# Input projection of a hybrid decoder: ten of thirteen tiles as Strassen pairs

## The chip, the cores and the metric

One core of a Trainium2 chip runs the whole program. The metric is the device time of one execution in microseconds (us), the median of several. TensorE multiplies matrices (PE in the profile; PEld is its weight load), VectorE (DVE), ScalarE (ACT) and GpSimd (POOL) do the elementwise work, SyncE (SP) issues most DMAs. Every engine works through its own queue in order and waits on semaphores. All data is float32.

## The reference

One inference step of a decoder trunk with 1024 prompt tokens and 8 sample tokens, 1032 in all. First the tokens are normalised, `xn = x * rsqrt(mean(x*x) + eps) * norm_g`, and projected, `u = xn @ w_in`, with 1024 input features. The first 1664 columns of `u` are `z`, the input of the RWKV branch:

```
zm = z + mu * (z_prev - z)
r, k, v, wl, al = split(zm)        # 512, 512, 512, 64, 64 columns
w_raw = -softplus(-(w0 + tanh(wl) @ w_b)) - 0.5
```

`z_prev` is `z` of the token before (zero before the first prompt token, a stored row for each sample token). The last row of `z` of the prompt and the rows of the samples, before mixing, are outputs. The RWKV recurrence, the sparse attention, the merge of the two and the rest of the trunk follow; the change doesn't touch them.

## The kernel before

The kernel is a row of stages, each ended by a barrier of all engines. The change is in the first, `project_input`, which makes `z` for all tokens, transposed: features on the 128 partitions, tokens along the free dimension. `zT` holds 13 tiles of 128 features by 1032 tokens. `Z_TILES` is the order of the tiles: tile 12 (the LoRA inputs wl and al) first, then k, r and v of each head pair.

The tokens arrive as nine tiles (eight of 128, one of 8). ACT sums the squares (L617) and takes the root, DVE scales the tile (L664), TensorE transposes it (`turn`, L552), eight transposes a tile, and ACT (L607) and DVE (L654) each copy half of the result out of PSUM into `xnT` and multiply it by the gain. ACT and DVE work in the order: square or scale tile i, then copy out tile i-1.

A product (`product`, L566) is one tile of `zT` for one third of the tokens: eight matmul calls, one for each 128 input features, 344 columns each. In float32 every call becomes two instructions, so 16 instructions in a product and 39 products in all. The order is

```
order = ([(n, g) for g in range(3) for n in range(Z_FIRST)] + [(n, g) for n in range(Z_FIRST, ZT) for g in range(3)])
```

with `Z_FIRST` = 4 (L431, L438): column group 0 of the first four tiles, then group 1, then group 2, while the later tokens are still on their way, and after those tile by tile. Behind each of the first six products stands the transposing of one token tile (L552), behind the ninth that of the stored shift rows (L584). Six PSUM banks go round; ACT copies each product out (L628) and, when a tile is complete, its last nine columns into `zlast` (L634).

The weights of a tile (`w_z`, 512 KB) come by DMA into a ring of four; SP asks for tile n when tile n-4 is done (`weights`, L491). POOL makes the difference `z_prev - z` of a complete tile (L538 to L540) and DVE mixes it in (L682). When all tiles are saved, TensorE transposes the 13 pieces of `zlast` (L589), ACT copies the rows out (L638), and SP stores them. The next stage, `rwkv_prompt`, begins with its LoRA products (L856, L858) and fills TensorE's gaps with the columns of the other branches (L845).

A much later stage, `merge_branches` (L2698 on), already computes its gates in quarter products: L2819 are its matmuls, L2835 ACT's copies, L2892 DVE's adds out of PSUM, L2860 the sums of weights and L2869 the sums of inputs, L2936 an addition on POOL.

Of the kernel before, what the change touches and what calls it, by code (L numbers as in the profile page):

```python
# [15 lines left out]
ALU = mybir.AluOpType  # L16
# [3 lines left out]
P = 128  # L20
# [410 lines left out]
Z_FIRST = 4  # L431
# [3 lines left out]
def project_input(nc, k, x, o):  # L435

    ring, w_ring = 4, 4
    order = ([(n, g) for g in range(3) for n in range(Z_FIRST)] + [(n, g) for n in range(Z_FIRST, ZT) for g in range(3)])  # L438
    place = {ng: u for u, ng in enumerate(order)}
    done_at = [1 + max(place[n, g] for g in range(3)) for n in range(ZT)]  # L440
    with Stage(nc) as ctx:
# [10 lines left out]
        d = sb("z_diff", [P, ring, TT])  # L452
        root_first = sb("root_first", [P, 1])
# [9 lines left out]
        diffed, mixed, lora_in = ctx.sem("z_diffed"), ctx.sem("z_mixed"), ctx.sem("tanh_done")  # L463
        block = ctx.enter_context(nc.Block())
# [20 lines left out]

        def turn_bank(i):
# [36 lines left out]
        def _(pool):  # L523
# [9 lines left out]
            for n, t in enumerate(Z_TILES):  # L533
                if n >= ring:
                    pool.wait_ge(mixed, n - ring + 1)
                pool.wait_ge(copied, done_at[n])
                s = d[:, n % ring, :]
                nc.gpsimd.tensor_scalar(s[:, 0:1], k.zT[:, t, 0:1], -1.0, None, ALU.mult).then_inc(diffed, 1)  # L538
                nc.gpsimd.tensor_tensor(s[:, 1:NP], k.zT[:, t, 0:NP - 1], k.zT[:, t, 1:NP], ALU.subtract).then_inc(diffed, 1)
                nc.gpsimd.tensor_tensor(s[:, NP:TT], st[:, t, :], k.zT[:, t, NP:TT], ALU.subtract).then_inc(diffed, 1)  # L540

        @block.tensor
        def _(pe):
# [12 lines left out]
            def product(u):  # L556
                n, g = order[u]
                if g == 0 or u >= 3 * Z_FIRST:
                    pe.wait_ge(in_w[n % w_ring], 16 * (n // w_ring + 1))
# [8 lines left out]
                last.then_inc(summed, 1)  # L568

# [6 lines left out]
            for u in range(len(order)):  # L576
                product(u)
                if u + 3 <= NT:
                    turn(u + 3)
                if u == NT:  # L580
                    pe.wait_ge(in_st, 16)
                    pe.wait_ge(out_v, NT + 1)
                    for t in range(ZT):
                        last = nc.tensor.transpose(k.ps[:, 7, t * NB:(t + 1) * NB], st_rows[:, t * P:(t + 1) * P],  # L584
                                                   k.ident[0:NB, 0:NB])
                    last.then_inc(st_t, 1)
            pe.wait_ge(saved, ZT)
            for t in range(ZT):
                last = nc.tensor.transpose(k.ps[0:NB + 1, t // 4, (t % 4) * P:(t % 4 + 1) * P], zlast[:, t, :],  # L589
                                           k.ident[:])  # L590
            last.then_inc(last_t, 1)

        @block.scalar
        def _(act):
# [31 lines left out]
            for u, (n, g) in enumerate(order):  # L626
                act.wait_ge(summed, u + 1)
                nc.scalar.activation(k.zT[:, Z_TILES[n], g * CG:(g + 1) * CG], k.ps[:, u % 6, 0:CG], ACT.Copy).then_inc(copied, 1)  # L628
                if g == 2:
                    act.wait_ge(copied, u + 1)  # L630
                    if n == Z_FIRST + 2:
                        act.wait_ge(mixed, 1)
                        nc.scalar.activation(k.zT[0:HD, ZT - 1, :], k.zT[0:HD, ZT - 1, :], ACT.Tanh).then_inc(lora_in, 1)
                    nc.scalar.activation(zlast[:, Z_TILES[n], :], k.zT[:, Z_TILES[n], NP - 1:TT], ACT.Copy).then_inc(saved, 1)  # L634
            act.wait_ge(last_t, 1)
            for b in range(4):
                n = min(4, ZT - 4 * b) * P
                nc.scalar.activation(k.last_rows[:, b * 512:b * 512 + n], k.ps[0:NB + 1, b, 0:n],  # L638
# [4 lines left out]
        def _(dve):  # L643
# [13 lines left out]

            dve.wait_ge(vec_o, 1)
# [11 lines left out]
            turned_out(NT)  # L670
            nc.vector.tensor_scalar(k.omka[:], k.vec[:, V_KA:V_KA + NPAIR], -1.0, 1.0, ALU.mult, ALU.add).then_inc(vec_o, 1)
# [7 lines left out]
            for n, t in enumerate(Z_TILES):  # L679
                dve.wait_ge(saved, n + 1)  # L680
                dve.wait_ge(diffed, 3 * n + 3)
                nc.vector.scalar_tensor_tensor(out=k.zT[:, t, :], in0=d[:, n % ring, :],  # L682
                                               scalar=k.vec[:, V_MU + t:V_MU + t + 1], in1=k.zT[:, t, :],
                                               op0=ALU.mult, op1=ALU.add).then_inc(mixed, 1)
# [2947 lines left out]
```

## Time and profile before

| | us |
|---|---|
| three timed runs | 1788.53, 1781.71, 1786.95 |
| their median | 1786.95 |
| the profiled execution | 1775.88 |
| its span in the profile | 1774.1 |
| TensorE busy (share of the span) | 1690.9 (95%) |
| DVE, ACT, POOL busy | 814.6, 577.2, 376.7 |
| matmuls of L566 busy | 182.0 |

The profile shows one execution. Busy time of TensorE counts the time in which at least one matmul is under way; matmuls overlap, so the mean length of one (453 ns for 344 columns) is longer than the step from one to the next. A row of the timeline gives the start, the length, the engine, the line, the operation with what it writes and reads, and in brackets how long the engine had been idle and what released it.

### The profile page before, as it was taken

What the parts mean: (1) busy time and instruction counts of PE and PEld (TensorE: products, weight loads), DVE (VectorE), ACT (ScalarE), POOL (GpSimd) and SP (SyncE); (2) the same over time, 40 slices, a digit from 0 to 9 for tenths busy, and PEclk for the clock granted to TensorE, in tenths of its full rate; (3) what the DMA queues carried; (4) which work ended last, traced back from release to release, by engine and by line L of the source; (5) the groups of instructions that cost most, each with busy time, mean ns of one, the idle gap of its engine ahead of it and who ended that gap; (6) DMA issues with size and microseconds to landing.
All of it is one profiled execution on the core that took longest, in us unless ns stands there. A gap on an engine that the chain in (4) does not pass through costs nothing. (4 is left out here: it accounts for less than half of the span.)

```text
span 1774.1 us, 40928 instructions
## 1 busy us (share of the span) xinstructions
PE 1690.9 (95%) x17848; PEld 1157.7 (65%) x17848; DVE 814.6 (46%) x1684; ACT 577.2 (33%) x1229; POOL 376.7 (21%) x442
## 2 busy tenths in 40 slices
PE   7999889999999989999999899899999999899997
PEld 5666566666666645667666689776568888545443
DVE  3100165455545419077666666272133356633444
ACT  4111245344343211276666221113322221111444
POOL 0211233232212100055655322103300013100110
PEclk9999899999999999999999899899999999999999
DMA  4112001000100045091200497529720141510001
GB/s 159 48 36 54 2 3 27 14 15 15 26 15 15 15 125 74 1 251 49 96 2 1 125 306 285 173 77 214 189 52 24 48 142 25 220 42 1 24 24 48
DMA packets 115463, 135.88 MB, mean 77 GB/s; under 512 B 48252, under 2 KB 97093, under 8 KB 110334
## 3 DMA queue, kind: packets, MB, share of 16 engines
q1 hardware_dynamic: 106034, 83.97, 17.2%
q0 software_dynamic: 9216, 49.29, 9.0%
q8 instruction: 142, 2.33, 0.6%
q14 instruction: 35, 0.29, 0.1%
q10 hardware_dynamic: 36, 0.01, 0.0%
HBM read 120.64 MB, written 16.62 MB: 77 GB/s over the span
## 5 line engine op out<-in xcount | busy, mean ns | idle before, releaser
L845 PE MATMUL ps<-xnT,rw_side_w 128*128 128x344 f32 x576 | 204.0, 479 | 0.0
L566 PE MATMUL ps<-xnT,w_z 128*128 128x344 f32 x624 | 182.0, 453 | 2.3 <-DVE xnT L654 1.3
L566 PEld LDWEIGHTS ps<-xnT,w_z 128*128 128x128 f32 x624 | 117.9, 190 | 62.9 <-issue 1.5
L1965 POOL TENSOR_SCALAR probs<-probs,row_sums,gates 128x63 f32<-128x63 f32 (+6 forms) x148 | 95.6, 662 | 229.8 <-DVE row_sums L1921 229.3
L845 PEld LDWEIGHTS ps<-xnT,rw_side_w 128*128 128x128 f32 x576 | 99.2, 191 | 40.3 <-issue 3.3
L2232 PE MATMUL ps<-xnT,zT 128*128 128x344 f32 x384 | 120.8, 463 | 0.0
L2232 PEld LDWEIGHTS ps<-xnT,zT 128*128 128x128 f32 x384 | 71.7, 194 | 36.0 <-issue 5.6
L278 PE MATMUL ps<-w_kv,xnT 128*128 128x396 f32 x256 | 89.6, 509 | 3.5 <-DMA w_kv<-in_w_in_dram 3.4
L1870 ACT ACTIVATE probs<-probs,neg_max 128x63 f32<-128x63 f32 (+6 forms) x148 | 87.5, 595 | 1.5 <-DVE neg_max L1911 1.5
L1817 PE MATMUL ps<-kT,zT 64*128 64x512 f32 (+3 forms) x384 | 73.7, 496 | 2.6 <-PEq L82 1.4
L278 PEld LDWEIGHTS ps<-w_kv,xnT 128*128 128x128 f32 x256 | 48.8, 194 | 40.7 <-DMA w_kv<-in_w_in_dram 7.8
L1844 PE MATMUL ps<-probsT,kvtok 128*64 128x128 f32 x1056 | 75.3, 280 | 0.0
L682 DVE SCALAR_TENSOR_TENSOR zT<-z_diff,vec,zT 128x1032 f32<-128x1032 f32 x13 | 16.8, 1294 | 126.2 <-POOL z_diff L540 113.5
L1830 PE MATMUL ps<-ident,probs 128*128 128x128 f32 (+1 forms) x460 | 68.1, 280 | 5.1 <-DVE probsT L1942 3.4
L1886 ACT ACTIVATE probsT<-ps 128x512 f32<-128x512 f32 (+1 forms) x80 | 45.9, 574 | 82.6 <-PE ps L1830 82.6
L1844 PEld LDWEIGHTS ps<-probsT,kvtok 128*64 128x64 f32 x1056 | 56.0, 136 | 24.0 <-issue 23.0
L2936 POOL TENSOR_TENSOR mT<-mT,gate_n 128x258 f32<-128x258 f32 x28 | 23.7, 854 | 218.0 <-DVE gate_n L2899 218.0
L1344 POOL TENSOR_TENSOR rw_Lb<-rw_Lm,level_mask 128x512 f32<-128x512 f32 x40 | 53.9, 1355 | 63.8 <-DVE rw_Lm L1513 38.8
L1942 DVE COPY probsT<-ps 128x512 f32<-128x512 f32 (+1 forms) x80 | 50.5, 632 | 36.0 <-PE ps L1830 35.1
L2835 ACT ACTIVATE zT<-ps 128x258 f32<-128x258 f32 x72 | 27.8, 387 | 109.0 <-PE ps L2819 86.2
L1830 PEld LDWEIGHTS ps<-ident,probs 128*128 128x128 f32 (+1 forms) x460 | 49.8, 140 | 17.9 <-issue 10.5
L628 ACT ACTIVATE zT<-ps 128x344 f32<-128x344 f32 x39 | 17.3, 464 | 132.7 <-PE ps L566 132.7
(560 smaller groups left out, 3263.7 us busy)
## 6 DMA issues: line engine op xcount, KB each, us to landing
w_z<-in_w_in_dram SPq DMA_DIRECT2D x13, 512.0 KB, 3.8
xnT_kept<-xnT SPq DMA_DIRECT2D x1, 4128.0 KB
x_tok<-in_x_prompt_dram SPq DMA_DIRECT2D x8, 512.0 KB
rw_side_w<-in_w_in_dram SPq DMA_DIRECT2D x16, 256.0 KB, 3.3
zT<-in_w_in_dram SPq DMA_DIRECT2D x8, 512.0 KB, 5.3
ring_k<-in_w_in_dram SPq DMA_DIRECT2D x8, 512.0 KB, 5.3
w_out<-in_w_out_dram SPq DMA_DIRECT2D x1, 4096.0 KB
h_tok<-in_x_prompt_dram SPq DMA_DIRECT2D x8, 512.0 KB, 8.4
```

Source lines behind the costliest of these rows:

```text
L278: last = nc.tensor.matmul(k.ps[:, u % 4, 0:half], k.xnT[:, c, i * P:(i + 1) * P], w[:, c, h * half:(h + 1) * half], start=(c == 0), stop=( ...
L566: last = nc.tensor.matmul(k.ps[:, u % 6, 0:CG], w[:, n % w_ring, c, :], k.xnT[:, c, g * CG:(g + 1) * CG], start=(c == 0), stop=(c == KC - 1))
L845: ins = nc.tensor.matmul(k.ps[:, SIDE_BANKS[g % 2], 0:CG], w.side[:, t % 2, c, :], k.xnT[:, c, g % 3 * CG:(g % 3 + 1) * CG], start=(c == 0 ...
L1344: nc.gpsimd.tensor_tensor(w.Lb[:, n % 2], w.Lm[:].rearrange("p q c n -> p (q c) n"), bc(k.tab["level_mask"][:, n + 1, :], 1, 8), ALU.mult) ...
L1817: last = nc.tensor.matmul(k.ps[:, 2 * (s % 2) + g, at:at + w], k.qT[half(g), j, i * P:(i + 1) * P], keys[half(g), t0:t0 + w], start=True, ...
L1830: last = nc.tensor.transpose(k.ps[0:m, 4 + pc % 2, (2 * b + g) * P:(2 * b + g + 1) * P], region(n, br, g, t * P, m), k.ident[:])
L1844: last = nc.tensor.matmul(k.ps[half(g), 6 + n % 2, 0:P], vals, pt[0:m, pc % NPT, (2 * b + g) * P:(2 * b + g + 1) * P], start=(br == 1 and ...
L1870: nc.scalar.activation(every, every, ACT.Exp, scale=-1.0, bias=neg_m[:, at:at + 1], accum_out=ls[:, at:at + 1]).then_inc(expd, 1)
L1886: nc.scalar.activation(to, src, ACT.Copy).then_inc(pt_a, 1)
L1942: nc.vector.tensor_copy(to, src).then_inc(pt_v, 1)
L1965: nc.gpsimd.tensor_scalar(every, every, ls[:, at:at + 1], k.gates[:, i, gate:gate + 1], ALU.mult, ALU.mult).then_inc(scaled, 1)
L2232: ins = self.nc.tensor.matmul(self.k.ps[:, self.banks[n % nb], 0:CG], self.w[:, t % 2, c, :], self.k.xnT[:, c, g * CG:(g + 1) * CG], start ...
```

## The change

The tiles of the order are now three first tiles, in full products as before, and ten more in five pairs. A pair (two tiles of 128 features, 1024 input features, 1032 tokens) is a product of 2 x 2 blocks: two tiles of outputs, two halves of the inputs, and tokens in quarters of 258. Each half i of the tokens has two quarters h. Seven block products, P1, P5, P6, P3, P2, P7 and P4 in that order, take the place of eight; each is four matmul calls of 258 columns. P6, P3, P7 and P4 are added in PSUM onto banks that hold earlier ones.

Added for it: DVE makes four sums of inputs once (`tx`, 128 x 2064 each, in the space of the token tiles) and four sums of weights for every pair (`sums`, 128 x 512 each); ACT copies four quarters of each half out of PSUM and DVE adds three. POOL's differences and DVE's mixes follow the complete tiles. The last tile's difference and mix are made by DVE alone, in two halves.

Moved: column group 1 starts after three products; the transposes of token tiles 5 and 8 stand in the middle of products 3 and 6; the shift rows are transposed after product 9, and the input sums, weight sums and vector tables stand ahead of their copy on DVE; the weights of tile 4 and later are asked for at other points; the 13 transposes of the last rows stand before the last quarter product.

The diff, cut to its core:

```diff
-Z_FIRST = 4
+Z_FIRST = 3
+Z_PAIRS = 5
+Z_PRODUCTS = ("P1", "P5", "P6", "P3", "P2", "P7", "P4")
...
-    ring, w_ring = 4, 4
-    order = ([(n, g) for g in range(3) for n in range(Z_FIRST)] + [(n, g) for n in range(Z_FIRST, ZT) for g in range(3)])
+    ring, w_ring, cq = 4, 4, TT // 4
+    order = [(n, g) for g in range(3) for n in range(Z_FIRST)]
...
             def weights(n):
-                if n >= w_ring:
+                if n >= w_ring + Z_FIRST:
+                    sp.wait_ge(q_ps, 14 * ((n - w_ring - Z_FIRST) // 2 + 1))
+                elif n >= w_ring:
                     sp.wait_ge(summed, done_at[n - w_ring])
...
-            for n, t in enumerate(Z_TILES):
+            for n, t in enumerate(Z_TILES[:-1]):
                 if n >= ring:
                     pool.wait_ge(mixed, n - ring + 1)
-                pool.wait_ge(copied, done_at[n])
+                p, j = divmod(n - Z_FIRST, 2)
+                if n < Z_FIRST:
+                    pool.wait_ge(copied, done_at[n])
+                elif j == 0:
+                    pool.wait_ge(q_add, 6 * p + 4)
+                else:
+                    pool.wait_ge(q_add, 6 * p + 6)
+                    pool.wait_ge(q_copy, 8 * p + 8)
...
                 for c in range(KC):
+                    if c == KC // 2 and u % 3 == 2 and u + 3 <= NT:
+                        turn(u + 3)
...
+            def pair_product(name, p, i):
...
+                bank = {"P5": 4 + i, "P3": 4 + i, "P2": 6 + i}.get(name, bank_a(p, i))
+                if name == "P1":
...
+                    if p >= 2:
+                        pe.wait_ge(q_copy, 8 * (p - 2) + 7 + i)
+                    else:
+                        pe.wait_ge(copied, plain)
+                elif name == "P5":
+                    pe.wait_ge(s_made, 4 * p + 1)
+                    pe.wait_ge(t_made, 1)
...
+                elif name == "P6":
+                    pe.wait_ge(s_made, 4 * p + 2)
+                    pe.wait_ge(t_made, 2)
+                    pe.wait_ge(q_copy, 8 * p + 1 + i)
+                elif name == "P3":
+                    pe.wait_ge(s_made, 4 * p + 3)
+                    pe.wait_ge(q_copy, 8 * p + 3 + i)
...
+                elif name == "P7":
+                    pe.wait_ge(s_made, 4 * p + 4)
+                    pe.wait_ge(t_made, 3)
+                    pe.wait_ge(q_copy, 8 * p + 5 + i)
+                else:
+                    pe.wait_ge(t_made, 4)
+                    pe.wait_ge(q_add, 6 * p + 5 + i)
+                for c in range(4):
+                    last = nc.tensor.matmul(k.ps[:, bank, 0:cq], left[:, c, :], right[:, c, :],
+                                            start=(c == 0 and name in ("P1", "P5", "P2")), stop=(c == 3), skip_group_check=True)
+                last.then_inc(q_ps, 1)
...
+            for p in range(Z_PAIRS):
+                for name in Z_PRODUCTS:
+                    for i in range(2):
+                        pair_product(name, p, i)
+                        if p == Z_PAIRS - 1 and name == "P4" and i == 0:
+                            last_rows()
...
+            def operand_sums(p, group):
...
+                    dve.wait_ge(in_w[n % w_ring], 16 * (n // w_ring + 1))
+                if p:
+                    dve.wait_ge(q_ps, 14 * (p - 1) + (6, 8, 12)[group])
...
+            def mix_last():
...
+                nc.vector.tensor_tensor(s[:, 1:mid], z[:, 0:mid - 1], z[:, 1:mid], ALU.subtract)
...
+                nc.vector.scalar_tensor_tensor(out=z[:, 0:mid - 1], in0=s[:, 0:mid - 1], scalar=mu, in1=z[:, 0:mid - 1],
+                                               op0=ALU.mult, op1=ALU.add)
+                dve.wait_ge(saved, ZT)
+                dve.wait_ge(q_copy, 8 * p + 8)
+                nc.vector.tensor_tensor(s[:, mid:NP], z[:, mid - 1:NP - 1], z[:, mid:NP], ALU.subtract).then_inc(last_d, 1)
...
+            for p in range(Z_PAIRS):
+                a, b = pair_tile(p, 0), pair_tile(p, 1)
+                added(p, a, 1, 7, 4, 5)
+                if p + 1 < Z_PAIRS:
+                    operand_sums(p + 1, 0)
+                    operand_sums(p + 1, 1)
+                added(p, a, 0, 9, 6, 1)
+                added(p, b, 1, 11, bank_a(p, 0), 3)
+                if p + 1 < Z_PAIRS:
+                    operand_sums(p + 1, 2)
+                for n in range(Z_FIRST) if p == 0 else range(2 * p + 1, 2 * p + 3):
+                    mix(n)
+            mix(ZT - 2)
+            mix_last()
```

## Rows read from the trace of the kernel before

**Rows 1.** The page: TensorE's busy time and its granted clock in 40 slices.

```profile
PE 1690.9 (95%) x17848; PEld 1157.7 (65%) x17848; DVE 814.6 (46%) x1684; ACT 577.2 (33%) x1229; POOL 376.7 (21%) x442
...
PEclk9999899999999999999999899899999999999999
```

**Rows 2.** Busy time (and instructions) of each engine in the stage's matmul stretch.

```profile
16.50:204.40 187.90, 186.85 (x685) 123.88 (x685) 28.52 (x55) 35.31 (x94) 26.74 (x36) 1.00 0.16 42
```

**Rows 3.** Groups by line, 0 to 260 us: busy us, mean ns, idle before.

```profile
L566 PE MATMUL ps<-xnT,w_z 128*128 128x344 f32 x624 | 182.0, 453 | 2.3 <-DVE xnT L654 1.3 <-ACT zT L628 1.0
L566 PEld LDWEIGHTS ps<-xnT,w_z 128*128 128x128 f32 x624 | 117.9, 190 | 62.9 <-issue 1.5 <-ACT xnT L607 1.1
L539 POOL TENSOR_TENSOR z_diff<-zT 128x1023 f32<-128x1023 f32 x13 | 24.5, 1887 | 0.0
...
L682 DVE SCALAR_TENSOR_TENSOR zT<-z_diff,vec,zT 128x1032 f32<-128x1032 f32 x13 | 16.8, 1294 | 126.2 <-POOL z_diff L540 113.5 <-ACT z_last L634 12.6
```

**Rows 4.** Timeline of the token transposes: start us, us, engine, line, operation.

```profile
24.60 0.75 DVE L664 TENSOR_SCALAR x_tok<-x_tok,x_sd 128x1024 f32<-128x1024 f32 x1
...
27.36 1.14 ACT L607 ACTIVATE xnT<-ps,vec 128x128 f32<-128x128 f32 x4 [3.00 <-PE ps L552]
...
27.60 4.79 PE L566 MATMUL ps<-xnT,w_z 128*128 128x344 f32 x16
```

**Rows 5.** Timeline around the last token transposes and the shift state.

```profile
48.83 0.66 PE L552 MATMUL ps<-ident,x_tok 8*128 8x8 f32 x8
...
49.89 2.21 ACT L628 ACTIVATE zT<-ps 128x344 f32<-128x344 f32 x6
...
50.51 14.12 PE L566 MATMUL ps<-xnT,w_z 128*128 128x344 f32 x48 [1.02 <-ACT zT L628]
...
64.56 0.96 PE L584 MATMUL ps<-ident,shift_rows 8*128 8x8 f32 x13
...
65.56 0.27 DVE L678 COPY shift_T<-ps 128x104 f32<-128x104 f32 x1 [14.42 <-PE ps L584]
```

**Rows 6.** Timeline of the stage's end.

```profile
204.56 0.46 ACT L628 ACTIVATE zT<-ps 128x344 f32<-128x344 f32 x1 [4.17 <-PE ps L566]
...
205.31 1.59 PE L589 MATMUL ps<-ident,z_last 128*9 128x128 f32 x13 [0.79 <-ACT z_last L634]
...
206.94 1.70 ACT L638 ACTIVATE last_rows<-ps 9x512 f32<-9x512 f32 x4 [1.68 <-PE ps L589]
...
209.04 0.31 SPq L520 DMA_DIRECT2D out_s_shift_dram<-last_rows  x1
...
210.97 1.19 PE L856 MATMUL ps<-zT,rw_lora 64*128 64x512 f32 x1 [4.07 <-PEq L82]
```

**Rows 7.** Windows over two units of the later stage, line 2819's instructions alone.

```profile
1338.50:1362.86 24.36, 24.36 (x113) 21.26 (x112) 1.00 0.18 44
```

**Rows 8.** Groups by line of that later stage, 1324 to 1399 us.

```profile
L2892 DVE TENSOR_TENSOR gate_n<-ps,zT 128x258 f32<-128x258 f32 x18 | 7.7, 427 | 46.0 <-PE ps L2819 46.0
...
L2835 ACT ACTIVATE zT<-ps 128x258 f32<-128x258 f32 x18 | 7.0, 387 | 28.5 <-PE ps L2819 28.5
L2860 DVE TENSOR_TENSOR zT<-ring_k 128x512 f32<-128x512 f32 x8 | 5.5, 684 | 1.4 <-PEq L82 1.4
L2869 DVE TENSOR_TENSOR w_out<-xnT,w_out 128x2064 f32<-128x2064 f32 x2 | 4.6, 2300 | 0.0
```

**Rows 9.** Timeline: DVE adds beside a POOL instruction in the later stage.

```profile
1472.22 1.11 POOL L2936 TENSOR_TENSOR mT<-mT,gate_n 128x258 f32<-128x258 f32 x1 [0.36 <-DVE gate_n L2899]
...
1472.66 0.41 DVE L2892 TENSOR_TENSOR zT<-ps,zT 128x258 f32<-128x258 f32 x1
```

**Rows 10.** Windows at the next stage's start; granted clock: third from last.

```profile
209.00:210.00 1.00, 0.00 (x0) 0.00 (x0) 0.00 (x0) 0.00 (x0) 0.00 (x0) 0.63 0.32 53
...
219.00:220.00 1.00, 1.00 (x4) 0.56 (x4) 0.00 (x0) 0.00 (x0) 0.76 (x1) 0.75 0.00 0
```

**Rows 11.** The tile w_z: its DMA transfers.

```profile
DMA to landing us min/median/max: 3.7/3.8/9.4
```

More of the change, by code:

```diff
@@ L484, in tokens, with pair_tile, pair_w, quarter @@
             return NB if i == NT else P
+        def pair_tile(p, j):
+            return Z_TILES[Z_FIRST + 2 * p + j]
+        def pair_w(p, j, half):
+            return w[:, (Z_FIRST + 2 * p + j) % w_ring, 4 * half:4 * half + 4, :]
+        def quarter(t, i, h):
+            return k.zT[:, t, (2 * i + h) * cq:(2 * i + h + 1) * cq]
+        def bank_a(p, i):
+            return 2 * (p % 2) + i
         def turn_bank(i):
@@ L570, in _, with last_rows @@
+            def last_rows():
+                pe.wait_ge(saved, ZT)
+                for t in range(ZT):
+                    last = nc.tensor.transpose(k.ps[0:NB + 1, 4 + t // 4, (t % 4) * P:(t % 4 + 1) * P], zlast[:, t, :],
+                                               k.ident[:])
+                last.then_inc(last_t, 1)
             pe.wait_ge(in_vec, 160)
@@ L656, in turned_out @@
                 last.then_inc(out_v, 1)
+            def operand_sums(p, group):
+                for j in range(2):
+                    n = Z_FIRST + 2 * p + j
+                    dve.wait_ge(in_w[n % w_ring], 16 * (n // w_ring + 1))
+                if p:
+                    dve.wait_ge(q_ps, 14 * (p - 1) + (6, 8, 12)[group])
+                if group == 0:
+                    nc.vector.tensor_tensor(sums[:, 0], pair_w(p, 1, 0), pair_w(p, 1, 1), ALU.add).then_inc(s_made, 1)
+                    dve.wait_ge(s_made, 4 * p + 1)
+                    nc.vector.tensor_tensor(sums[:, 1], sums[:, 0], pair_w(p, 0, 0), ALU.subtract).then_inc(s_made, 1)
+                elif group == 1:
+                    dve.wait_ge(s_made, 4 * p + 2)
+                    nc.vector.tensor_tensor(sums[:, 3], pair_w(p, 0, 1), sums[:, 1], ALU.subtract).then_inc(s_made, 1)
+                else:
+                    nc.vector.tensor_tensor(sums[:, 2], pair_w(p, 0, 0), pair_w(p, 1, 0), ALU.subtract).then_inc(s_made, 1)
@@ new lines, in added, with mix @@
+            def added(p, to, h, group, bank, held):
+                for i in range(2):
+                    dve.wait_ge(q_ps, 14 * p + group + i)
+                    dve.wait_ge(q_copy, 8 * p + held + i)
+                    z = quarter(to, i, h)
+                    nc.vector.tensor_tensor(z, k.ps[:, bank + i, 0:cq], z, ALU.add).then_inc(q_add, 1)
+            def mix(n):
+                t = Z_TILES[n]
+                dve.wait_ge(saved, n + 1)
+                dve.wait_ge(diffed, 3 * n + 3)
+                nc.vector.scalar_tensor_tensor(out=k.zT[:, t, :], in0=d[:, n % ring, :],
+                                               scalar=k.vec[:, V_MU + t:V_MU + t + 1], in1=k.zT[:, t, :],
+                                               op0=ALU.mult, op1=ALU.add).then_inc(mixed, 1)
@@ L670, in _ @@
             turned_out(NT)
+            dve.wait_ge(turned, 2 * (NT + 1))
+            dve.wait_ge(out_a, NT + 1)
+            for n in range(4):
+                dve.wait_ge(t_made if n else out_v, n if n else NT + 1)
+                to, one, other = ((tx[:, 0], xv[:, 0:4, :, 1, :], xv[:, 0:4, :, 0, :]), (tx[:, 1], xv[:, 4:8, :, 1, :], tx[:, 0]),
+                                  (tx[:, 2], xv[:, 4:8, :, 1, :], xv[:, 0:4, :, 1, :]),
+                                  (tx[:, 3], xv[:, 4:8, :, 0, :], tx[:, 1]))[n]
+                nc.vector.tensor_tensor(to, one, other, ALU.subtract).then_inc(t_made, 1)
+                if n == 1:
+                    operand_sums(0, 0)
+                    operand_sums(0, 1)
+            operand_sums(0, 2)
             nc.vector.tensor_scalar(k.omka[:], k.vec[:, V_KA:V_KA + NPAIR], -1.0, 1.0, ALU.mult, ALU.add).then_inc(vec_o, 1)
@@ L678, in _ @@
             nc.vector.tensor_copy(st[:], k.ps[:, 7, 0:ZT * NB].rearrange("p (a b) -> p a b", b=NB)).then_inc(st_o, 1)
[L679 to L684, printed above, removed]
+            for p in range(Z_PAIRS):
+                a, b = pair_tile(p, 0), pair_tile(p, 1)
+                added(p, a, 1, 7, 4, 5)
[10 more added lines that the diff above has]
+            mix_last()
 LEVELS = (2, 4, 8, 16, 32)
```

79 lines of the change are left out of this document (57 added, 22 removed).

## The prediction

> **What bounds the kernel now.** I read the page first. TensorE is busy 95% of the span and its granted clock is at 8 tenths or above in every slice of it (the digit 9 is 90% or more) [rows 1], so a stage costs what its matmuls cost plus the holes between them. Then the stage that the change touches. It runs from the first product at 16.5 us to the next stage's first matmul at 210.97 us [rows 6]; between 16.5 and 204.4 us TensorE is busy for 186.85 of 187.90 us [rows 2], all at full clock, while DVE, ACT and POOL are busy for 28.5, 35.3 and 26.7 us. TensorE is the bound; the other engines have more than four fifths of their time free. The groups by line then say what the matmuls are: 39 products of 16 instructions, 624 in all, each of 344 columns, and 182.0 us of busy time [rows 3]. Undisturbed a product takes 4.63 us: ACT's copy behind each is 0.46 us of work after 4.17 us of waiting for TensorE [rows 6].
>
> **Part 1, quarter products in place of full ones.** Removed: 30 of 39 products (tiles 4 to 13 of the order), 30 x 4.63 = 138.9 us. Added: five pairs of 14 quarter products, 4 calls of 258 columns each. The kernel already has this very pattern in a later stage (same seven products in two halves, of the same size, with the same adds on DVE), and a window over one unit of it, 14 products, is 24.36 us long and all of it busy, 112 weight loads beside it [rows 7]. So 5 x 24.36 = 121.8 us, and the term is **-17.1 us**. Check from the other side: 344 columns x 8 calls in 4.63 us is 1.682 ns a column, 56 calls x 258 columns x 1.682 = 24.31 us, so nothing is lost by the shorter instruction. Ends: -17.4 us by the column rate; above, whatever TensorE waits for operands, which is the next point.
>
> What TensorE waits for inside a pair. P5 needs the first weight sum and the first input sum, P6, P3 and P7 the others; P6, P3 and P7 add onto banks that ACT must have copied; P4 needs DVE's add of P7. A quarter product takes 24.36/14 = 1.74 us. ACT's copies have three products (5.2 us) of slack for 0.39 us of work [rows 8]: nothing. P4 of half 0 comes only one product (1.74 us) after the end of P7 of half 0, and DVE's add takes 0.43 us [rows 8]; with 0.2 us allowed for the signal that is 0.65 us against 1.74, if DVE is free. What is queued on DVE ahead of it: two adds of P3, three weight sums for the next pair (3 x 0.68 us), two adds of P2. Counted from the end of P3, these end at about 0.6 + 2.1 + 0.9 = 3.6 us, and P7 of half 0 ends at 5.2 us. DVE is free 1.6 us before. I take 0; the other end is 1 us in each pair, 5 us.
>
> DVE and POOL side by side. POOL's difference of the pair's first tile (1.89 us, [rows 3]) starts when P2's adds are done and so lies over the add that P4 needs. In the later stage a DVE add with one input in PSUM took 0.41 us in the middle of a POOL instruction [rows 9], so it is not held: cost 0. Even a held add would end 2.9 us after P2, before the 3.48 us at which P4 is due.
>
> **Part 2, the first pair's operands.** New on DVE before it: four input sums over 2064 elements, 2.30 us each, and four weight sums of 0.68 us [rows 8], 12 us. DVE is free from the end of its token copies, about 48 us. The weights of the pair's second tile are now asked for after product 7 (about 54 us) and land 3.8 us later, at worst 9.4 us [rows 11], so at 58 us DVE goes on: three weight sums to 60, input sums to 65, the last weight sum to 65.7, the vector tables (1.2 us) to 66.9, then the state copy that POOL and P2 wait for, 67.1. When they are due: pair 1 starts at about 64.6 (below), P5 at 68.1, P6 at 71.6, P2 at 78.5, P7 at 82. The nearest is 7 us away, and a landing at the 9.4 us end moves it to 2 us or so. Cost 0; upper end 1 us. The wait that P1 itself gets, for ACT's copy of the last full product, ends 0.6 us after the product, under the 13 small transposes of 0.96 us that stand there as before [rows 5]. Later pairs: weights are asked for as the pair before last ends and DVE first needs them 12 to 14 us later. Nothing.
>
> **Part 3, three tiles first instead of four.** Column group 1 now begins after three products, not four, and needs token tile 5, so its transposes go into the middle of product 3; likewise those of the last tokens into product 6. For the first: product 3 starts at 27.60, its middle is 29.9; tile 5 was normalised at 24.60 + 0.75 us, and the earlier copies end at 28.5 [rows 4]. Transposes until 30.9, copies of 1.14 us until about 32.1, group 1 starts at about 33.1: no wait. For the second there is a gain. Before, product 7 waits 1.02 us for ACT [rows 5], because ACT turns to product copies only when the last tokens are done (49.89 us), and those are transposed only after product 6. Now they are transposed 2.5 us earlier, ACT starts copying at about 47.7, under product 6, and product 7 needs no wait: **-1.0 us** (ends 0 and -1.0: a wait cannot save more than it is).
>
> **Part 4, the end of the stage.** Before, from ACT's last product copy (204.56) to the next stage's first matmul 6.41 us pass: copy, 13 transposes of 1.59 us, ACT's four copies 1.70 us, two DMA issues until 209.35, barrier 1.6 us [rows 6]; POOL's difference and DVE's mix of the last tile end at 208.8. Now the 13 transposes stand before the last quarter product: +1.6 us in front of its end. They wait for the last column copies, which follow P7's add by 0.4 us while P4's half takes 1.74 us: no wait. After the end: ACT copy 0.39, its four copies 1.70, two DMA issues 0.65, barrier 1.6, together 4.45 us from ACT's last copy: -1.95 us. DVE's last half beside it: difference 0.6 and mix 0.75 us after that copy, done 2.0 us after ACT's copy starts; its first half follows mixes 10 to 12 (3 x 1.29 us, [rows 3]) and is done 0.8 us after it, so even then 2.3 us, before SP's 2.85. Net **-0.35 us** (ends -1.0 and +1.0).
>
> **Part 5, the clock behind the stage.** After TensorE's pause at the stage's end (206.9 to 210.97) its granted clock falls within 209 to 210 us and is full again within 219 to 220 [rows 10]: about 8.5 us of the next stage at 1.2 GHz. The pause is now 4.6 us long instead of 4.1. I take the same loss, so 0; ends -4.3 us (the whole stretch at 2.4 GHz, half of 8.5) and +4.3 us.
>
> **Sum.** -17.1 - 1.0 - 0.35 = -18.4 us. The profiled execution took 1775.88 us (span 1774.1), so 1757.5 us for such an execution. That one lies 11 us under the median of the three timed runs, 1786.95 (1781.71 to 1788.53); from the median the forecast is 1768.5 us. The stages behind are bound by TensorE too, and no DMA of theirs waits on a time fixed by something else: the side weights and LoRA loads are asked for some 50 us before their use. So the gain is kept.
>
> **Rivals.**
> 1. P4 waits for DVE's add in every pair. For: it is the only new wait with a single product of slack, and DVE's queue holds ten instructions a pair. Against: the 1.6 us that DVE is free ahead of it. If DVE were 2 us late in each: +10 us, about 1778. Chance 0.06.
> 2. Weight loads not hidden behind the shorter matmuls. For: there are now 560 in place of 480. Against: in the later stage 21.26 us of loads lie inside 24.36 us of matmuls [rows 7], in this one 117.9 beside 182.0 in 187.9 us. If they stood in line: 480 x (0.292 + 0.189) = 231 us before, 560 x (0.2175 + 0.190) = 228 after, a gain of 3 us, 1783 with the rest. Chance 0.02. The Trainium skill (TensorE: Matmul & The Clock Gate, "The mechanism") states that a weight load overlaps matmuls in flight only when its row group differs, and here it never differs. By that rule the time would be this rival's; the trace disagrees with the rule in both stages.
> 3. Slower than before: DVE stops in its queue for the weights of the next pair, with the adds of P2 and P7 behind it, so P4 and ACT's last copies stop TensorE. It decides only when the two loads land more than about 17 us after being asked for, in the pairs 3, 4 and 5, and outweighs the gain above 17 + 18.4/3 = 23 us. The longest landing of this tile was 9.4 us [rows 11]. With 25 us it is 3 x 8 = 24 us lost against 18.4 won, 1792.5 us. Chance 0.02.
> 4. The change saves more: the clock does not fall at the stage's end. 1764 us. The shorter tail speaks for it, the pause that is 0.5 us longer against it. Chance 0.05.
>
> **How the numbers follow.** Forecast 0.85. 0.5% is 9 us here, about what can be told from no change. Faster by more than that: the forecast, rival 4 and most of its bounds, 0.93; within: rivals 1 and 2 in part, 0.05; slower 0.02. The range: 1768.5 with the clock's 4.3 us and the timed runs' own spread of 3 to 5 us down to 1760, up with rival 1 and the spread to 1778.
>
> **What would show it.** Per pair, 112 instructions in 24.4 us without a wait of TensorE on DVE; no wait of product 7 on ACT; last rows' transposes ahead of the last four calls; next stage's first matmul at about 192.5 us instead of 210.97, and everything behind it earlier by the same 18.4 us. Wrong would be: waits of TensorE on DVE's adds or sums, quarter products at more than 1.76 us, or a later stage that gives time back.

## The result, and the profile after

| | before | after |
|---|---|---|
| median of the timed runs, us | 1784.53 (4 runs, 1781.71 to 1788.53) | 1757.26 (4 runs, 1754.59 to 1758.24) |
| ratio, 95% interval | | 0.9871 [0.9834, 0.9907] |
| the profiled execution, us | 1775.88 | 1757.08 |
| its span, us | 1774.1 | 1755.3 |

The change is faster. The forecast was 1768.5 us (1760 to 1778) from the first three runs of before, a ratio of 0.9897. Of the two profiled executions it said 18.4 us less, and they are 18.8 us apart. The timed runs gave 27 us in this comparison, which puts the median 2.7 us under the range; on another chip, with more runs (experiment e1), the ratio was 0.9895 [0.986, 0.9929]. Lines behind the stage are numbered 171 higher after; L600 are now the full products, L646 the quarter products, L653 the last rows, L1027 the next stage's first matmul.

The page after: TensorE's busy time fell by 17.0 us, its share and its clock did not move [rows 1].

```profile
PE 1673.9 (95%) x17928; PEld 1172.7 (67%) x17928; DVE 849.1 (48%) x1743; ACT 578.5 (33%) x1239; POOL 373.0 (21%) x439
...
PEclk9999899999999999999999899899999999999999
```

Windows of the kernel after: length, busy time of PE, PEld, DVE, ACT and POOL with their instructions, then TensorE's granted clock. The first is the whole stage, the second one pair of tiles, the others lie in the next stage. The pair is like [rows 7]: 24.36 us, all busy, 112 loads beside it.

```profile
15.84:191.50 175.66, 171.36 (x778) 140.09 (x779) 64.76 (x115) 39.36 (x111) 27.10 (x36) 1.00 0.18 46
...
90.11:114.47 24.36, 24.36 (x113) 21.26 (x112) 7.46 (x12) 5.86 (x12) 4.89 (x7) 1.00 0.16 43
192.00:200.00 8.00, 8.00 (x58) 5.78 (x56) 3.07 (x7) 4.21 (x6) 3.51 (x3) 0.50 0.01 2
...
201.00:202.00 1.00, 1.00 (x6) 0.75 (x5) 0.00 (x0) 0.40 (x2) 0.00 (x0) 1.00 0.00 0
```

The starts of pairs 1, 2 and 3 in TensorE's timeline of the kernel after, 24.46 and 24.36 us apart; pairs 3 and 4 take 24.36 us too:

```profile
63.71 3.75 PE L646 MATMUL ps<-xnT,w_z 128*128 128x258 f32 x16
...
88.17 3.64 PE L646 MATMUL ps<-xnT,w_z 128*128 128x258 f32 x16
...
112.53 3.64 PE L646 MATMUL ps<-xnT,w_z 128*128 128x258 f32 x16
```

A pair in the timeline of the kernel after, DVE's queue against TensorE's (start, length, engine, line, operation, idle time before and its releaser):

```profile
79.82 0.69 DVE L768 TENSOR_TENSOR z_sums<-w_z,z_sums 128x512 f32<-128x512 f32 x1
80.43 0.42 DVE L778 TENSOR_TENSOR zT<-ps,zT 128x258 f32<-128x258 f32 x1
...
81.21 3.64 PE L646 MATMUL ps<-x_tok,z_sums 128*128 128x258 f32 x16
81.41 0.43 DVE L778 TENSOR_TENSOR zT<-ps,zT 128x258 f32<-128x258 f32 x1 [0.57 <-PE ps L646]
...
82.10 1.89 POOL L571 TENSOR_TENSOR z_diff<-zT 128x1023 f32<-128x1023 f32 x1
83.15 0.43 DVE L778 TENSOR_TENSOR zT<-ps,zT 128x258 f32<-128x258 f32 x1 [1.31 <-PE ps L646]
...
84.69 3.64 PE L646 MATMUL ps<-x_tok,w_z 128*128 128x258 f32 x16
```

The first add of P7 starts at 83.15, after DVE had been idle for 1.31 us, and the P4 calls that need it start at 84.69, 1.1 us after its end. The first add of P2 (80.43) stands right behind a weight sum, the second (81.41) already waited for TensorE.

What TensorE waited for from the first product to the next stage in the kernel after (us in all, times, longest): two rows, the wait that the first product ends and the one at the stage's end. Before, the same view had two more, L566 on ACT 1.0 us and L589 on ACT 0.8 us [rows 5, 6]. There is none on DVE's adds.

```profile
PE ps L1027 <- PEq L82: 4.3, 1, 4.3
PE ps L600 <- DVE xnT L751: 1.5, 1, 1.5
```

The end of the stage in the timeline of the kernel after, against [rows 6]:

```profile
183.87 1.58 PE L653 MATMUL ps<-ident,z_last 128*9 128x128 f32 x13
...
185.29 1.91 PE L646 MATMUL ps<-x_tok,w_z 128*128 128x258 f32 x8
...
187.23 0.39 ACT L731 ACTIVATE zT<-ps 128x258 f32<-128x258 f32 x1 [2.77 <-PE ps L646]
189.60 0.31 SPq L545 DMA_DIRECT2D out_s_shift_dram<-last_rows  x1
...
191.50 1.19 PE L1027 MATMUL ps<-zT,rw_lora 64*128 64x512 f32 x1 [4.30 <-PEq L82]
...
201.38 1.40 PE L1016 MATMUL ps<-xnT,rw_side_w 128*128 128x344 f32 x4
```

From ACT's last copy to the next stage 4.27 us pass, 6.41 before. Where the 18.8 us are, by the same marks in both traces:

| from | to | before | after | difference | forecast |
|---|---|---|---|---|---|
| first product | first matmul behind the shift rows' transposes | 48.9 (16.5 to 65.5) | 47.9 (15.8 to 63.7) | -1.1 | -1.0 |
| there | ACT's last product copy | 139.1 | 123.5 | -15.6 | -17.1 + 1.6 |
| there | next stage's first matmul | 6.41 | 4.27 | -2.1 | -1.95 |
| there | first matmul of the stage after that | 433.6 | 434.3 | +0.7 | 0 |

The first product came 0.7 us earlier, which is start-up and not the change (it lies between 15.5 and 16.7 us in all the runs below). So the next stage starts 19.5 us earlier, and from the stage after it (644.5 and 625.8 us) on every stage does so by 18.1 to 18.8 us, to the end. The stage itself is 18.8 us shorter; the next stage's 0.7 us more and the start-up's 0.7 us less happen to cancel.

### The profile page after: what moved, and what is told of

Read it like the earlier page. It is cut to its first block and busy times, and to the rows that moved or that the text cites. A ratio compares the mean times of both kernels' runs of the same rounds, so it can differ in the third digit from the quotient of the medians.

```text
span 1755.3 us, 41208 instructions
## 1 busy us (share of the span) xinstructions
PE 1673.9 (95%) x17928; PEld 1172.7 (67%) x17928; DVE 849.1 (48%) x1743; ACT 578.5 (33%) x1239; POOL 373.0 (21%) x439
## 5 line engine op out<-in xcount | busy, mean ns | idle before, releaser
L3220 PE MATMUL ps<-w_sums,ring_k 128*128 128x512 f32 x128 | 57.2, 593 | 1.4 <-DVE h_tok L3533 1.4
L2990 PE MATMUL ps<-xnT,zT 128*128 128x258 f32 x256 | 57.6, 381 | 0.0
L1754 DVE SCALAR_TENSOR_TENSOR rw_SC<-ps,rw_ends,rw_XT 128x64 f32<-128x64 f32 x64 | 18.2, 284 | 77.7 <-PE ps L1297 77.7
L646 PE MATMUL ps<-x_tok,z_sums 128*128 128x258 f32 x240 | 53.8, 381 | 0.0
```

Of the source, the lines that this page charges most:

```text
L646: last = nc.tensor.matmul(k.ps[:, bank, 0:cq], left[:, c, :], right[:, c, :], start=(c == 0 and name in ("P1", "P5", "P2")), stop=(c == 3) ...
L2990: last = nc.tensor.matmul(k.ps[:, bank, 0:CQ], stationary(u, n, name, c), moving(u, n, name, c, i), start=(c == 0 and name in ("P1", "P5", ...
L3220: last = nc.tensor.matmul(k.ps[:, bank, :], left[:, c, :], right[:, c, :], start=(first and c == 0), stop=(c == 3), skip_group_check=True)
```

## The experiments

Times of stages are read from each run's one profile. "Stage" is from the first product to the next stage's first matmul: 194.45 us before, 175.66 after.

**e1_changed: the kernel after again**, beside before, in more runs (no edit).

> The changed kernel as it is, timed in turn with the kernel before. Theory (the sum of the prediction: 17.1 us fewer columns, 1.0 us of a wait gone, 0.35 us in the tail): 18 to 19 us faster, ratio 0.9895. Rival, drawn from the first runs (medians 27 us apart, ratio 0.9871): there is a further gain of some 5 us or more that the traces, 18.8 us apart, don't show; ratio 0.987 or below.

Measured: 1761.31 us (12 runs, 1751.26 to 1774.92) against 1780.21 (23 runs, 1770.48 to 1792.54), ratio 0.9895 [0.986, 0.9929]. Stage 175.7 us, next stage 434.5 us. This ratio is the traces' 18.8 us (1757.1/1775.9 = 0.9894), and it lies inside the first comparison's interval, so a further gain isn't shown. The rival's 0.987 lies inside this interval, so it isn't ruled out either. One place where single runs differ stands under the last heading.

**e3_fill_only and e2_tail_fill: the pause at the stage's end.** e3 adds six matmuls after the last pair, whose result nobody reads; e2 adds four and shortens the tail: ACT copies the last rows before its last product copy, and DVE leaves only 260 columns of the last tile for the end.

```diff
+            for c in range(6):
+                nc.tensor.matmul(k.ps[:, 2, 0:cq], pair_w(0, 0, 0)[:, c % 4, :], xv[:, c % 4, 0, 0, :], start=(c == 0),
+                                 stop=(c == 6 - 1), skip_group_check=True)
```

In e2 the loop is `range(4)`, and further, first on ACT, then on DVE (the halves of the last tile are cut at 3 * cq likewise):

```diff
+                    if p == Z_PAIRS - 1 and i:
+                        act.wait_ge(last_t, 1)
+                        for c in range(4):
+                            n = min(4, ZT - 4 * c) * P
+                            nc.scalar.activation(k.last_rows[:, c * 512:c * 512 + n], k.ps[0:NB + 1, 4 + c, 0:n],
+                                                 ACT.Copy).then_inc(last_o, 1)
...
+                if p == Z_PAIRS - 1:
+                    mix(2 * p + 1)
+                    mix(2 * p + 2)
```

> The changed kernel with nothing but six further matmul calls (258 columns, result unused, 2.6 us) on TensorE behind the last product, so that its pause is 1.7 us instead of 4.3. The end of the stage stays where it is. Theory: the clock does not fall, next stage 2 to 4.5 us shorter. Rival: no change, or the clock falls all the same: 0.

> The changed kernel with a shorter end of the stage: ACT copies the last rows before the last quarter product instead of behind it, DVE mixes tiles 10 and 11 of the order at the start of the last pair and only 260 columns behind the last copy, and TensorE gets four further matmul calls (258 columns, result unused) behind the last product. Theory: the stage's end comes 1.3 us earlier (DVE's last mix becomes the last event, about 0.4 + 0.45 + 0.45 us after ACT's last copy starts), and since TensorE's pause shrinks from 4.3 to about 1.3 us the granted clock does not fall to half for the first 9 us of the next stage: 2 to 4.5 us more, 3 to 6 us in all. Rival (the clock falls at its own time, or the first 9 us of that stage hang on the chain through ACT and DVE, not on TensorE's clock): 1.3 us in all.

Windows of e3, then of e2, over the same places as above:

```profile
192.00:195.00 3.00, 3.00 (x53) 2.64 (x50) 0.73 (x1) 2.95 (x5) 0.00 (x0) 0.88 0.02 5
195.00:198.00 3.00, 3.00 (x7) 1.76 (x6) 2.78 (x7) 1.29 (x2) 1.62 (x2) 0.56 0.00 0
198.00:202.00 4.00, 4.00 (x47) 2.38 (x45) 1.20 (x2) 3.18 (x6) 3.18 (x3) 1.00 0.00 0
```

```profile
190.00:193.00 3.00, 2.14 (x20) 1.72 (x20) 0.00 (x0) 2.13 (x3) 0.00 (x0) 1.00 0.03 8
193.00:198.00 5.00, 4.81 (x48) 3.02 (x48) 3.51 (x7) 3.65 (x6) 2.29 (x2) 1.00 0.00 0
```

The timeline of e2's end:

```profile
187.80 0.39 ACT L740 ACTIVATE zT<-ps 128x258 f32<-128x258 f32 x1
...
188.68 0.49 DVE L814 SCALAR_TENSOR_TENSOR zT<-z_diff,vec,zT 128x260 f32<-128x260 f32 x1
...
190.86 0.66 PE L1038 MATMUL ps<-zT,rw_lora 64*128 64x512 f32 x1 [1.36 <-PEq L82]
...
196.74 1.40 PE L1027 MATMUL ps<-xnT,rw_side_w 128*128 128x344 f32 x4
```

TensorE pauses 4.30 us after, 1.69 in e3 and 1.36 in e2. The granted clock of the next stage is at 0.50 for 8 us and more after, low in part of 192 to 198 us in e3, and 1.00 throughout in e2: the level 2.4 GHz is kept. The next stage takes 434.3 us after, 427.9 in e3 and 428.7 in e2. What of it is the clock's is read from the next stage's first matmul to the side matmuls that start just after the clock is full again in the kernel after: 9.88 us after (191.50 to 201.38), 5.88 in e2 (190.86 to 196.74), and 7.06 in e3. So the filled pause gives 4.0 us in e2 and 2.8 in e3, as both expectations had it. The rest of the difference (1.6 us in e2, 3.5 in e3) arises later, where the clock is full in all three. It need not be the pause's: e9 below, whose pause of 4.3 us isn't filled and whose clock falls as after, has a next stage of 430.4 us, 3.8 us shorter, and is 0.1 us longer up to that same mark. Without a filled pause the next stage took 430.4 to 434.6 us in nine traces; what moves it isn't known. The shorter tail alone is worth 1.2 us (stage 174.5 us in e2, 175.7 in e3). Timed, e3 has 0.9877 [0.9839, 0.9915] (10 runs) and e2 0.9874 [0.9824, 0.9924] (6 runs); e1's 0.9895 lies inside both. So the trace shows e2 7 us ahead of the kernel after at the start of the stage after the next one (603.2 against 610.0 us from the first product), and the timed runs don't tell them apart.

**e4_turns_behind: the moved transposes back.** The transposes of the last tokens stand behind product 6 and the last rows behind all pairs, as before.

```diff
-                    if c == KC // 2 and u % 3 == 2 and u + 3 <= NT:
+                    if c == KC // 2 and u == 2:
...
-                        if p == Z_PAIRS - 1 and name == "P4" and i == 0:
-                            last_rows()
+            last_rows()
```

> Two moves of the change undone: the transposes of the last tokens stand behind product 6 again, and the 13 transposes of the last rows behind the last quarter product. Theory: product 7 waits 1.0 us for ACT's first copy, and from ACT's last product copy to the next stage's first matmul it is 6.3 us instead of 4.3, with 1.6 us less in front of it: 0.35 us lost there, 1.4 us in all. Rival (the wait on ACT was something else, the first copies being late anyway): 0.4 us in all.

```profile
50.07 6.31 PE L600 MATMUL ps<-xnT,w_z 128*128 128x344 f32 x21 [1.03 <-ACT zT L712]
```

Further down the same timeline:

```profile
187.12 0.39 ACT L730 ACTIVATE zT<-ps 128x258 f32<-128x258 f32 x1 [1.35 <-PE ps L646]
...
188.54 1.70 ACT L734 ACTIVATE last_rows<-ps 9x512 f32<-9x512 f32 x4 [1.03 <-PE ps L653]
...
192.54 1.19 PE L1026 MATMUL ps<-zT,rw_lora 64*128 64x512 f32 x1 [4.04 <-PEq L82]
```

The wait of 1.03 us of [rows 5] is back, and with it the first part is 48.9 us in place of 47.9. At the end the transposes cost nothing ahead of the last copy (122.1 us from the first pair on, 123.5 after) but 1.15 us behind it (5.42 against 4.27 us). Moving them ahead is no gain, it costs 0.25 us: TensorE has to do them either way. Stage 176.5 us, +0.8: the 1.03 us came as expected, but the end won 0.25 us where a loss of 0.35 was expected (1.4 us in all). What shortened the tail from 6.41 to 5.42 us is that the last columns of the last tile are copied before its last quarter: TensorE's idle 0.79 us of [rows 6] is gone.

**e5_dve_late: DVE's add comes later and later.** 0, 2, 4, 6 and 8 additions of 512 columns, of no use, stand before DVE's add of P7 in pairs 1 to 5.

```diff
+                for _ in range((0, 2, 4, 6, 8)[p]):
+                    dve.wait_ge(pad_done, npad[0])
+                    nc.vector.tensor_tensor(flat_x[:, 8704:9216], k.xnT[:, 0, 0:512], k.xnT[:, 1, 0:512], ALU.add).then_inc(pad_done, 1)
+                    npad[0] += 1
```

> The changed kernel with further DVE instructions (512 elements, result unused, about 0.7 us each with its own wait) between DVE's adds of P2 and of P7: none in the first pair, then 2, 4, 6 and 8. It shows how late DVE may be before P4 has to wait. Theory: P7's add of the first half is over at 83.58 us and P4 starts at 84.69, and DVE is idle 1.3 us ahead of that add, so about 2.3 us are free: pairs of 24.4, 24.4, 25.0, 26.4 and 27.9 us, 6 us in all. Rival 1 of the prediction (the slack is far smaller, DVE's lag comes through from the start): 1.4, 2.9, 4.3 and 5.8 us, 14 us in all.

Timeline of e5, pair 2 and then pair 3; L853 are the additions:

```profile
106.58 3.15 DVE L853 TENSOR_TENSOR x_tok<-xnT 128x512 f32<-128x512 f32 x2
...
107.30 1.88 POOL L572 TENSOR_TENSOR z_diff<-zT 128x1023 f32<-128x1023 f32 x1
...
110.22 3.72 PE L647 MATMUL ps<-x_tok,w_z 128*128 128x258 f32 x16 [0.54 <-DVE zT L779]
```

```profile
131.72 4.61 DVE L853 TENSOR_TENSOR x_tok<-xnT 128x512 f32<-128x512 f32 x4
...
136.81 5.41 PE L647 MATMUL ps<-x_tok,w_z 128*128 128x258 f32 x16 [1.99 <-DVE zT L779]
```

```profile
137.00:140.00 3.00, 3.00 (x9) 2.45 (x9) 3.00 (x3) 0.30 (x2) 0.00 (x0) 0.59 0.00 0
140.00:143.00 3.00, 3.00 (x13) 2.47 (x13) 0.00 (x1) 0.69 (x2) 0.18 (x2) 0.84 0.00 0
```

The additions took 3.15, 4.61, 6.06 and 7.51 us. P4 starts 3.48 us after P7 in an undisturbed pair (81.21 and 84.69 above). In pairs 2 and 3 P7 started at 106.03 and 131.17, so P4 was 0.71 and 2.16 us late, in pairs 4 and 5, read the same way, 3.60 and 5.05. Always it is the additions' length less 2.45 us: that is the slack of DVE's add, 1.31 us idle before it and 1.1 behind. Pair 1, with no addition, took 24.46 us, pairs 2 to 4 took 25.14, 28.28 and 28.04. Pair 3 lost 3.92 us to an add that was 2.16 us late; the rest is the clock, at 0.59 in 137 to 140 us, where the sixteen P4 calls took 5.41 us in place of 3.64. In pair 4, with the longer wait, the clock stayed at 1.00, and in the last pair it fell again.

The stage took 190.65 us, 15.0 more than after. The expectation of 6 us missed, and the rival's 14 us is met in size only: the slack of 2.45 us is there. Two things that the expectation left out make the difference. The first two additions took 3.15 us where it allowed 1.4 (see below, on DVE beside POOL), which is 1.7 us in each of four pairs, and the fallen clock added some 3.5 us in pairs 3 and 5.

**e6_narrow: shorter quarter products.** Pairs 1 to 5 compute 258, 224, 192, 128 and 64 columns; the rest of `z` is left out.

```diff
-                    last = nc.tensor.matmul(k.ps[:, bank, 0:cq], left[:, c, :], right[:, c, :],
+                    last = nc.tensor.matmul(k.ps[:, bank, 0:w_cols(p)], left[:, c, :], right[:, c, 0:w_cols(p)],
```

> The changed kernel with quarter products over fewer columns: 258 in the first pair, then 224, 192, 128 and 64, the rest of each quarter left out of the computation. It shows when the weight loads stop being hidden. Theory A (a load overlaps the matmul before it and has a step of its own of 0.11 to 0.13 us, as in the token transposes, eight in 1.04 us): 0.218, 0.189, 0.163 us an instruction, then 0.11 to 0.13 for 128 and 64 columns; pairs of 24.4, 21.2, 18.2, 12 to 15 and 12 to 15 us. Theory B (a load takes its 0.190 us of the profile and only then the next): 24.4, 21.3, 21.3, 21.3, 21.3. Rival 2 of the prediction (loads and matmuls in line): 45 us in the first pair, 30 in the last.

Timeline of e6, TensorE alone (the columns stand behind 128x):

```profile
119.62 2.76 PE L649 MATMUL ps<-xnT,w_z 128*128 128x192 f32 x16
122.22 2.76 PE L649 MATMUL ps<-x_tok,z_sums 128*128 128x192 f32 x16
...
132.78 1.95 PE L649 MATMUL ps<-xnT,z_sums 128*128 128x128 f32 x16
134.56 1.95 PE L649 MATMUL ps<-xnT,w_z 128*128 128x128 f32 x16
...
142.08 3.74 PE L649 MATMUL ps<-x_tok,z_sums 128*128 128x64 f32 x32
145.66 0.61 PE L649 MATMUL ps<-xnT,z_sums 128*128 128x64 f32 x4
```

Two quarter products of 192 columns take 2.60 us (119.62 to 122.22), of 128 columns 1.78; four of 64 columns take 3.58, or 1.79 for two. An instruction then costs 0.2175 us at 258 columns, 0.1625 at 192 and 0.112 at both 128 and 64 (pairs of 24.5, 21.2, 18.2, 12.9 and 14.0 us, the last with the 13 transposes in it: theory A), a floor that no longer depends on the columns, with one load to each instruction. (Whether the load or the issue of a pair sets it, isn't separated.) At 258 columns a load is hidden with 0.1 us to spare, so rival 2 is out. The rule of the Trainium skill (TensorE: Matmul & The Clock Gate, "The mechanism") that a load overlaps matmuls in flight only when its row group differs does not hold here: with the same rows throughout, a load and a matmul in line would take 0.112 + 0.2175 us, 36.9 us a pair, and the pair takes 24.36. The same section of the Trainium skill also lets a load into the background weight buffer be pulled ahead of matmuls in flight; whether that is what happens here, no run shows.

**e7_last_by_pool: the last tile as all others,** its difference on POOL and one mix on DVE.

```diff
-            for n, t in enumerate(Z_TILES[:-1]):
+            for n, t in enumerate(Z_TILES):
...
-            mix_last()
+            mix(ZT - 1)
```

> The changed kernel with the last tile treated like the others: POOL makes its difference when the whole tile is there and DVE mixes it in one instruction, in place of DVE's two halves. Theory: behind ACT's last copy stand 2.3 us of POOL and 1.3 us of DVE, ending 1.3 us after SP's stores are issued, and the next stage starts 1.3 us later. Rival (the stores or the barrier end the stage anyway): 0.

```profile
189.22 0.31 SPq L545 DMA_DIRECT2D out_s_shift_dram<-last_rows  x1
...
189.75 1.30 DVE L784 SCALAR_TENSOR_TENSOR zT<-z_diff,vec,zT 128x1032 f32<-128x1032 f32 x1 [3.76 <-POOL z_diff L572]
...
192.49 1.19 PE L1027 MATMUL ps<-zT,rw_lora 64*128 64x512 f32 x1 [5.68 <-PEq L82]
```

In this timeline SP has issued its last DMA at 189.53 and DVE's mix ends at 191.05, so DVE sets the end. Stage 177.0 us, +1.4: that is what the mixing in halves is worth, and without it part 4 would be 0.7 us of loss (-0.7 + 1.4).

**e8_late_weights: the price of rival 3.** SP asks for a pair's weights ten products later.

```diff
-                    sp.wait_ge(q_ps, 14 * ((n - w_ring - Z_FIRST) // 2 + 1))
+                    sp.wait_ge(q_ps, 14 * ((n - w_ring - Z_FIRST) // 2 + 1) + 10)
```

> The changed kernel with the weights of pairs 3, 4 and 5 asked for ten quarter products later (17.4 us). It gives the price of rival 3 of the prediction, DVE held in its queue by a load. Theory: the loads land some 7 us after being asked for, at 24.5 us of the pair before; DVE then makes three sums (2.1 us) and the adds of P2 and P7 (1.3 us), so P4 starts at 28 us instead of 20.9: 7 us in each of three pairs, 21 us, which outweighs the whole gain of the change. Rival (DVE catches up, or only P1 of the next pair waits): 3 us or less in each.

Timeline of e8 in pair 2:

```profile
106.45 0.99 SPq L519 DMA_DIRECT2D w_z<-in_w_in_dram  x2
112.20 0.69 DVE L763 TENSOR_TENSOR z_sums<-w_z 128x512 f32<-128x512 f32 x1 [8.80 <-DMA w_z<-in_w_in_dram]
...
115.59 6.22 PE L646 MATMUL ps<-x_tok,w_z 128*128 128x258 f32 x16 [5.69 <-DVE zT L778]
```

The weights land 5.7 us after being asked for, DVE stands 8.80 us at its first weight sum, the adds of P2 and P7 behind it are late, and P4 waits 5.69 us. Three pairs took 32.8, 31.7 and 33.1 us, 24.5 us lost (21 were expected) for 17.2 us of waiting; again the clock fell at each wait (0.50 in 115 to 119 us) and P4 took 6.22 us. The stage took 200.2 us, 5.7 more than before the change. So the mechanism of rival 3 is real and can outweigh the gain. Its threshold follows: P4 started 9.34 us after P7 (106.25 in this trace), 5.86 late, with weights that landed 17.4 + 5.7 us after the usual time of asking, so up to 17.2 us nothing is lost. The forecast said 17.

**e9_eight: eight for eight.** P1 is computed twice.

```diff
-                for c in range(4):
+                for c in (0, 1, 2, 3, 0, 1, 2, 3) if name == "P1" else range(4):
```

> The changed kernel with the calls of P1 made twice in every pair (same result), so that eight block products are made where eight would be needed, and all else stays. Theory: each pair takes 27.84 us instead of 24.36 (two quarter products more at 1.74), the next stage starts 17.4 us later, and against the kernel before only the wait of product 7 and the tail are left: 1 to 2 us faster, ratio 0.999. Rival (part of the gain comes from something else in the new order of work): clearly below, 0.995 or less.

Window over one pair, and the waits of TensorE in a much later stage, both of e9:

```profile
67.61:95.45 27.84, 27.84 (x129) 24.32 (x128) 8.66 (x13) 3.51 (x11) 10.28 (x14) 1.00 0.09 24
```

```profile
PE ps L2236 <- issue: 21.3, 1, 21.3
```

A pair takes 27.84 us, 3.48 more, five times 17.4; the stage takes 193.1 us, 1.4 less than before. So in the trace all but 1.4 us of the stage's gain comes from the product that is left out, and the seven others lose nothing by their order or their adds.

The timed ratio of 0.999 that was expected missed: it is 1.0057 [1.003, 1.0085] (9 runs), 5 to 15 us slower than the kernel before, where the stage is 1.4 us shorter. The profile shows why for its own execution: one halt of 21.3 us in a stage that the change doesn't touch. Whether the other eight runs had it too isn't known, and the lowest of the nine is 1782.82 us. So the reading rests on the stage's length in one trace, and the timed runs' loss is open.

**e10_before_fill: the kernel before, its pause filled.**

```diff
+            pe.wait_ge(copied, 3 * ZT - 1)
+            for c in range(4):
+                nc.tensor.matmul(k.ps[:, 4, 0:CG], w[:, 0, c, :], k.xnT[:, c, 0:CG], start=(c == 0), stop=(c == 3))
```

> The kernel before with four further matmul calls of 344 columns (2.3 us, result unused) on TensorE behind the transposes of the last rows, so that its pause there is 1.7 us instead of 4.1. It shows whether what the clock costs behind the stage is the same before and after the change. Theory: it is, and was there before: from the next stage's first matmul to the first of the stage behind it 427 to 429 us instead of 433.5, 5 to 6 us faster. Rival (the clock falls in both, or the loss belongs to the change): 0.

```profile
209.00:215.00 6.00, 5.00 (x60) 3.84 (x60) 2.23 (x3) 4.73 (x6) 0.96 (x1) 1.00 0.02 4
```

```profile
PE ps L859 <- PEq L82: 1.8, 1, 1.8
```

The pause is 1.75 us in place of 4.07, the clock stays at 1.00, and the next stage takes 429.7 us in place of 433.6, 3.9 us less where 5 to 6 were expected. Of these, 3.6 us are gained by the mark used for e2 and e3 (5.87 us from the next stage's first matmul on, 9.45 before). Timed: 1780.03 against 1783.15 us, ratio 0.9984 [0.9951, 1.0016] (10 runs), which can't be told from no change. The clock's share is thus about the same with and without the change, 4.0 us (e2) and 3.6 us (e10) with the clock kept, and no part of its gain.

## Why the prediction was right

- **Part 1** (-17.1 us): right, -17.0 (the table's -15.6 less the transposes' 1.4). The first pair took 24.46 us, those behind it 24.36, the later stage's unit, and TensorE never waited for DVE. e9's trace shows that the product left out is the gain, e6 that the columns set the time and not the loads.
- **DVE's slack**: 1.6 us free before P7's end by the forecast, 1.31 measured; with P4's product behind it 2.4, and e5 finds the same edge by moving the add.
- **DVE beside POOL**: right for the add out of PSUM, 0.43 us at 83.15 inside POOL's 1.89 us. In e5 the additions with both inputs in SBUF are held: each two more cost 1.45 us, 0.73 apiece, but the first two took 3.15, so 1.7 us are on top, about the length of POOL's instruction (1.88 us at 107.30). The Trainium skill (SBUF — State Buffer, "SBUF: two separate sides") says that a GpSimd operation that reads SBUF and a DVE operation with two SBUF inputs take a shared pair of ports in turn, each for a whole instruction; the trace agrees, in both kinds.
- **Part 2** (0): right; pair 1 starts at 63.71 us and nothing waits.
- **Part 3** (-1.0): right, -1.1; e4 brings the 1.03 us back.
- **Part 4** (-0.35): mis-sized, -0.7. The tail was 4.27 us for 4.45 (the terms that the forecast names add up to 4.34), and the transposes ahead of it 1.4 for 1.6. The reason given for the gain was partly wrong: not the moved transposes (e4: +0.25) but the last columns' copy, which no longer stands behind the last product (e4). DVE's halves were needed to keep it (e7: 1.4 us).
- **Part 5** (0, with ends of 4.3): right. The clock fell after a pause of 4.30 us (forecast 4.6) as it had before, and the next stage took 0.7 us longer, well within the 4 us by which it differs between traces. The end of 4.3 us, half of 8.5, has the right size: 4.0 us came back in e2 and 3.6 in e10, where the clock was kept.
- **Rivals**: 1 and 4 did not occur; 2 is refuted by e6 and the pairs' 24.36 us (its 0.292 us for a full instruction should be 4.63/16 = 0.289, a gain of 2 us in place of 3); 3 is shown to exist in e8, and far away.
- **The range**: the stage's 18.8 us meet the forecast's 18.4 by its own terms. That the two whole executions also differ by 18.8 is partly luck: the gathering stage of the last heading took 139.1 us before and 139.2 after, and 137.2 to 161.7 in the other traces. The absolute forecast missed its range by 2.7 us in the first comparison: it was tied to a median of three runs of before, 1786.95, where 23 later runs have 1780.21. The spread of a timed run was taken as 3 to 5 us and is 10 to 14 to either side (e1).

## What to carry to other kernels

When a kernel already contains the pattern that a change brings, one window over one unit of it is a better price than any sum of durations. What such a change can lose is found in the in-order queues: count the slack of the one operand that is due a single product later, and ask what stands ahead of it on its engine, DMA waits included. A short wait of TensorE costs more than its length where the clock falls behind it, and a pause at a barrier can be filled with a few idle matmuls (some 4 us in the traces here, which the timed runs are too few to tell). Compare traces stage by stage: the stages that a change doesn't touch differ between executions by more than such a gain.

## What the runs showed of the hardware

- A pause of 4.1 to 4.3 us at the stage's end was followed by 8.5 (before) to 9.4 us (after) at 1.2 GHz; with the pause cut to 1.36 us (e2) or 1.75 us (e10) the clock stayed at 2.4 GHz, with 1.69 us (e3) it fell for part of 6 us, so the pause's length alone doesn't decide. Inside the matmul stretch five of six waits of 1.99 to 6.0 us (e5, e8) came with some 3.4 to 6.8 us at 1.2 GHz. The sixth, 3.44 us in pair 4 of e5, was not, nor was one of 0.54 us. Why the sixth wasn't stays open.
- A load of 128 columns and its matmul go through in 0.112 us (e6), below the 0.190 us that the load alone is shown with.
- Executions of one kernel differ by 20 us and more. Four traces show one place: TensorE stood 21.3 us in e9 (above), 8.2 in e6, 6.3 in e7 and 6.0 in e2 in the stage that gathers cache chunks by indirect DMA, beside a wait of 6.5 us that every kernel has there; the other eight traces have no second wait of that kind. From its first matmul to the next stage's it took 161.7 us in e9, 148.3 in e2 and 139.2 after. What held the gathering wasn't tried.
